# Gate rows summed by TensorE inside the norm transitions, and twelve modulation units of four rows of 512 in feed-forward blocks zero and one

## The reference, cut to what matters

```python
sh1, sc1, gt1, sh2, sc2, gt2 = split(silu(c) @ w_ada + b_ada, 6)
x = x + gt1 * mixer(rmsnorm(x, g_mix) * (1 + sc1) + sh1)
x = x + gt2 * swiglu(rmsnorm(x, g_ffn) * (1 + sc2) + sh2)     # feed-forward block zero
x = rmsnorm(x, g_final)
(sh1, sc1, g1, sh2, sc2, g2, sh3, sc3, g3) = split(silu(c_2) @ w_ada_2 + b_ada_2, 9)
x = x + 0.5 * g1 * swiglu(mod(x, sh1, sc1))                   # feed-forward block one
x = x + g2 * (attention_mixer(mod(x, sh2, sc2)) @ w_out_2)
x = x + 0.5 * g3 * swiglu(mod(x, sh3, sc3))                   # feed-forward block two
out = rmsnorm(x, final_norm_2)
```

## Time and profile before

| | us |
|---|---|
| median of 3 runs (1157.52 to 1158.29) | 1157.75 |
| profiled execution, its own time from first to last instruction (the span) | 1156.4 |
| TensorE busy with matmuls / weight loads | 1118.4 / 1008.5 |
| VectorE, ScalarE, POOL busy | 853.4, 571.7, 74.7 |
| HBM traffic | 250.29 MB, mean 216 GB/s |

### The profile page before, as it was taken

How to read it: one execution, slowest core, us unless ns; L and a number is a source line. 1 busy time by engine, 2 the same in 40 slices (tenths; PEclk the granted TensorE clock), 3 DMA queues, 4 the chain that set the end, 5 groups by cost and what they waited for, 6 DMA issues and landing times.

```text
span 1156.4 us, 19131 instructions
## 1 busy us (share of the span) xinstructions
PE 1118.4 (97%) x7744; PEld 1008.5 (87%) x7744; DVE 853.4 (74%) x1082; ACT 571.7 (49%) x733; POOL 74.7 (6%) x143
## 2 busy tenths in 40 slices
PE   2999999999999999999999999999999999999997
PEld 2899988999999888888788888889999998888885
DVE  1578766897777688877888778878777776755676
ACT  3495434544434644445454454446655546444442
POOL 4000000100000100000200000011000001000001
PEclk8899999999999999999999999999999999999999
DMA  9934554688875488778468777747965654655771
GB/s 287 291 114 140 188 175 154 183 273 263 296 233 187 154 282 272 238 247 293 154 226 271 252 258 263 239 152 240 292 183 182 222 178 165 218 182 191 234 247 37
DMA packets 192548, 250.29 MB, mean 216 GB/s; under 512 B 4859, under 2 KB 171966, under 8 KB 192350
## 3 DMA queue, kind: packets, MB, share of 16 engines
q1 hardware_dynamic: 183838, 216.92, 57.8%
q0 software_dynamic: 8640, 32.38, 8.4%
HBM read 248.23 MB, written 1.05 MB: 216 GB/s over the span
## 4 chain that ended last, share of the span: by engine, by line
PE 87%; DVE 7%; ACT 2%; SPq 2%; DMA 1%; issue 1%; POOL 0%; POOLq 0%; DVEq 0%; ACTq 0%
PE twin L1291 85%; DVE wlo L1912 2%; DVE arena L1920 2%; DMA arena<-in_w_ada 1%; DVE arena L1912 1%; ACT arena L862 1%; DVE X L1912 1%; ACT whi L862 1%; PE twin L1628 1%; SPq L520 1%; SPq L570 0%; DVE arena L1916 0%; PE twin L1749 0%; PE twin L1416 0%; DVE B_lo L1912 0%
## 5 line engine op out<-in xcount | busy, mean ns | idle before, releaser
L1291 PE MATMUL twin<-A_both,whi 128*128 128x256 f32 (+1 forms) x2208 | 578.7, 339 | 3.1 <-DVE A_both L1912 1.6
L1912 DVE TENSOR_TENSOR wlo<-raw,whi 128x2048 fp32r<-128x2048 f32 (+1 forms) x171 | 386.9, 2263 | 117.1 <-ACT whi L862 117.0
L1291 PE MATMUL twin<-A_both,wlo 128*128 128x256 f32 x1632 | 436.5, 280 | 0.0
L862 ACT ACTIVATE whi<-raw 128x2048 fp32r<-128x2048 f32 x169 | 323.2, 1913 | 206.8 <-PE twin L1291 205.7
L1291 PEld LDWEIGHTS twin<-A_both,whi 128*128 128x128 f32 x2208 | 370.1, 190 | 46.1 <-issue 7.9
L1291 PEld LDWEIGHTS twin<-A_both,wlo 128*128 128x128 f32 x1632 | 309.2, 189 | 11.4 <-DVE A_both L1912 0.6
L1920 DVE SCALAR_TENSOR_TENSOR arena<-ada_raw,arena 128x256 f32<-128x256 f32 (+2 forms) x322 | 167.3, 520 | 15.9 <-issue 1.7
L862 ACT ACTIVATE arena<-twin 128x512 f32<-128x512 f32 (+5 forms) x171 | 90.8, 556 | 111.5 <-PE twin L1291 81.9
L862 ACT ACTIVATE arena<-arena 128x512 f32<-128x512 f32 (+7 forms) x132 | 69.9, 559 | 149.1 <-DVE arena L1912 116.0
L1291 PE MATMUL twin<-whi,B_hi 128*128 128x512 f32 (+2 forms) x340 | 126.6, 372 | 0.2 <-DVE B_lo L1912 0.2
L1291 PE MATMUL twin<-wlo,B_hi 128*128 128x512 f32 (+2 forms) x340 | 125.1, 368 | 0.0
(11 more groups left out here) (137 smaller groups left out, 900.6 us busy)
## 6 DMA issues: line engine op xcount, KB each, us to landing
raw<-in_w_in SPq DMA_DIRECT2D x48, 1024.0 KB, 5.7
raw<-in_ffn_w_in SPq DMA_DIRECT2D x44, 1024.0 KB, 5.1
ada_raw<-in_w_ada POOLq DMA_DIRECT2D x28, 1024.0 KB, 6.0
ada_raw<-in_w_ada SPq DMA_DIRECT2D x24, 1024.0 KB, 5.4
raw<-in_w_ffn_in SPq DMA_DIRECT2D x22, 1024.0 KB, 5.1
raw<-in_ffn_w_out SPq DMA_DIRECT2D x22, 1024.0 KB, 5.0
raw<-in_w_ffn_out SPq DMA_DIRECT2D x11, 1024.0 KB, 5.0
arena<-in_w_ada SPq DMA_DIRECT2D x8, 1024.0 KB, 11.8
```

What stands on the lines that cost most here:

```text
L862: return nc.scalar.activation(o, i, f, **kw)
L1291: return nc.tensor.matmul(o, l, r, start=start, stop=stop, **kw)
L1912: return nc.vector.tensor_tensor(o, x, y, op)
```

## The change

The gate sums leave their five places. `gate_half(r, 0)` runs in the norm transition behind `shift_and_scale`, `gate_half(r, 1)` behind the transposes, each in a bank that stays untouched until `gate_row(r)` has read it; r = 1, 2, 3, 4 go to norm 2, 3, 4, 5, and r = 0 behind the transposes of the last ga unit. `gate_row` of r = 1, 2, 4 moves on DVE from the end of the block to its beginning, that of r = 3 to the third unit of the second mixer; it now waits for `gr_in` itself. TensorE waits for `gr_done` in the middle of the second up unit of each block and before uq. The `keep_warm` products go, but for eight in norm 3. The column sums move to bank 0 (bank 7 for norm 4). All modulation units become half pairs of four rows of 512; blocks zero and one take twelve each, at the slots `ADA_STEP` (1, 3, 6, 8, 11, 13, 16, 18, 21, 23, 26, 28, counted three to a step), block two none. SP and DVE write all steps out; ACT and PE keep the loops, now also for all of block two.

```diff
@@ -113,22 +113,19 @@
     ADA += [(_blk, _col * D + 256 * n) for n in range(4)]
-NADA1, NADAF, NADA2 = 16, 10, 12
+NADA1, NADAF, NADA2 = 16, 12, 12
 ADA_P2 = NADA1 + 2 * NADAF
-ADA_LAST = ADA_P2 + NADA2
+ADA_STEP = [1 + 5 * j // 2 for j in range(NADAF)]
 MOD_STEP = {4: 0, 5: 1, 7: 2, 9: 3, 11: 4, 13: 5, 16: 6, 18: 7, 21: 8, 24: 9, 26: 10, 28: 11, 30: 12, 32: 13, 34: 14, 36: 15}
-ADA_FFN = [n for n in range(len(ADA)) if NADA1 <= n < ADA_P2 or n >= ADA_LAST]
+ADA_FFN = [n for n in range(len(ADA)) if NADA1 <= n < ADA_P2]
 ADA_MIX = [n for n in range(len(ADA)) if n not in ADA_FFN]
-LAST_STEPS = (0, NF - 4, NF - 3, NF - 2)
-
-
 def ada_pos(n):
-    return n if n < NADA1 else n - NADA1 if n < ADA_P2 else n - ADA_P2
+    return n if n < NADA1 else (n - NADA1) % 20
@@ -462,14 +459,11 @@
-        def feed_forward_steps(eng, f, step):
-
-            end = NF - 1 if f < 2 else NF - 4
-            with eng.Fori(0, (end - 1) // 3) as j:
+        def feed_forward_steps(eng, step):
+
+            with eng.Fori(0, (NF - 2) // 3) as j:
                 for m in range(1, 4):
                     step((j, m), m)
-            for i in range(end, NF - 1):
-                step(i, i)
@@ -498,13 +492,10 @@
         def ada_source(n):
-            if ADA_P2 <= n < ADA_LAST:
-                blk, c0 = ADA[n - n % 2]
-                k = 4 * (n % 2)
-                return a["w_ada_2"][0].rearrange("(p k) n -> p k n", k=KD)[:, k:k + 4, c0:c0 + 2 * UC]
-            blk, c0 = ADA[n]
-            w = a["w_ada"][0] if blk == 0 else a["w_ada_2"][0]
-            return w.rearrange("(p k) n -> p k n", k=KD)[:, :, c0:c0 + UC]
+            blk, c0 = ADA[n - n % 2]
+            k = 4 * (n % 2)
+            w = a["w_ada"] if blk == 0 else a["w_ada_2"]
+            return w[0].rearrange("(p k) n -> p k n", k=KD)[:, k:k + 4, c0:c0 + 2 * UC]
@@ -534,32 +525,28 @@
-                def piece(a, i, b, n):
-
-                    if isinstance(i, tuple):
-                        return bass.ds(lin(a, i, b), n)
-                    return slice(a * i + b, a * i + b + n)
-
-                def step(i, m):
-                    load(u0 + 2, i, w_in[:, :, piece(UC, i, UC, UC)], KD)
-                    load(u0 + 3, i, w_in[:, :, piece(UC, i, DFF + UC, UC)], KD)
-                    load(u0 + 4, i, w_out[:, piece(2, i, 0, 2), :], 2)
-                    if f < 2:
-                        n0 = NADA1 + NADAF * f
-                        blk, c0 = ADA[n0 + m]
-                        w = (a["w_ada"] if blk == 0 else a["w_ada_2"])[0].rearrange("(p k) n -> p k n", k=KD)
-                        if n0 == NADA1 and m == 0:
-                            sp.wait_ge(*ada_done(n0 - 1))
-                        else:
-                            sp.wait_ge(ada_mac, lin(KD, i, KD * ada_order(n0)))
-                        sp.dma_start(ada_raw[:], w[:, :, piece(UC, i, c0 - UC * m, UC)]).then_inc(ada_landed, 16)
-                    elif m in LAST_STEPS and i == m:
-                        load_ada(ADA_LAST + LAST_STEPS.index(m))
+                def next_ada(q):
+
+                    if f < 2 and q in ADA_STEP[:-1]:
+                        load_ada(NADA1 + NADAF * f + ADA_STEP.index(q) + 1)
+
+                def step(i):
+                    cs = slice(UC * i + UC, UC * i + 2 * UC)
+                    load(u0 + 2, i, w_in[:, :, cs], KD)
+                    next_ada(3 * i - 4)
+                    load(u0 + 3, i, w_in[:, :, DFF + UC * i + UC:DFF + UC * i + 2 * UC], KD)
+                    next_ada(3 * i - 3)
+                    load(u0 + 4, i, w_out[:, 2 * i:2 * i + 2, :], 2)
+                    if f < 2 and i == 0:
+                        load_ada(NADA1 + NADAF * f)
+                    next_ada(3 * i - 2)
                 load(u0, 0, w_in[:, :, 0:UC], KD)
                 load(u0 + 1, 0, w_in[:, :, DFF:DFF + UC], KD)
-                step(0, 0)
-                feed_forward_steps(sp, f, step)
+                step(0)
+                for i in range(1, NF - 1):
+                    step(i)
+                next_ada(3 * (NF - 1) - 4)
                 load(u0 + 3 * NF - 1, 0, w_out[:, 2 * (NF - 1):2 * NF, :], 2)
@@ -638,11 +625,11 @@
-            return 7 if n in (3, 4) else 3
-
-        def gate_bank(r):
-
-            return {0: 6, 3: 2}.get(r, 4)
+            return 7 if n == 4 else 0
+
+        def gate_bank(r, x):
+
+            return ((2, 3), (3, 4), (7, 3), (1, 3), (3, 5))[r][x]
@@ -780,7 +767,7 @@
                     pool.wait_ge(unit_used, 1)
-                pool.dma_start(ada_half if n >= ADA_P2 else ada_raw[:], ada_source(n)).then_inc(ada_landed_p, 16)
+                pool.dma_start(ada_half, ada_source(n)).then_inc(ada_landed_p, 16)
@@ -1341,12 +1328,17 @@
                 src = norm_source(n)
+                r = n - 1
+                if n == 3:
+                    pe.wait_ge(x_piece, 1)
                 shift_and_scale(n, column_bank(n))
-                warm = {2: 4, 5: 5}.get(n, 3)
+                if n == 4:
+                    pe.wait_ge(x_piece, 6)
+                gate_half(r, 0)
+                if n == 3:
+                    keep_warm(6, 8)
                 for t in range(TT):
-                    if t == 0:
-                        keep_warm(7 if n in (2, 5) else 6, {2: 4, 3: 16}.get(n, 5))
-                    else:
+                    if t:
                         turn_sums(n, column_bank(n))
@@ -1358,17 +1350,21 @@
                             ins.then_inc(tr_done, 1)
-                keep_warm(warm, 3)
-
-            def gate(r):
+                if n in (3, 4):
+                    pe.wait_ge(x_piece, 4 * (n - 2))
+                else:
+                    pe.wait_ge(x_ready, 1 if n == 2 else 5)
+                gate_half(r, 1)
+
+            def gate_half(r, x):
                 g0 = GATE_UNITS[r]
-                pe.wait_ge(*ada_done(g0 + 3))
-                pe.wait_ge(gr_in, 16 * (r + 1))
-                for x in range(2):
-                    c = UC * ada_pos(g0) + 512 * x
-                    ins = mm(bank[gate_bank(r) + x][:], ones[:], acc[:, c:c + 512], True, True)
-                ins.then_inc(gr_mm, 1)
+                if x == 0:
+                    pe.wait_ge(*ada_done(g0 + 3))
+                c = UC * ada_pos(g0) + 512 * x
+                ins = mm(bank[gate_bank(r, x)][:], ones[:], acc[:, c:c + 512], True, True)
+                if x:
+                    ins.then_inc(gr_mm, 1)
@@ -1548,10 +1544,12 @@
-                def up(u, i, b):
+                def up(u, i, b, gates=0):
                     pe.wait_ge(lo_ready, lin(3, i, u + 1))
                     for half in range(2):
+                        if half and gates:
+                            pe.wait_ge(gr_done, gates)
                         for k in range(KD):
@@ -1592,14 +1590,13 @@
                 first_up(u0, 0, low_count(2 + f + (f == 2)))
-                up(u0 + 1, 0, 2)
+                up(u0 + 1, 0, 2, (2, 3, 5)[f])
                 up(u0 + 2, 0, 4)
                 up(u0 + 3, 0, 6)
                 pe.wait_ge(prod_done, n0 + 1)
                 down(u0 + 4, 0, 0, True, False)
-                feed_forward_steps(pe, f, step)
+                feed_forward_steps(pe, step)
                 pe.wait_ge(prod_done, n0 + NF)
-                gate((1, 2, 4)[f])
                 down(u0 + 2, NF - 1, NF - 1, False, True)
@@ -1659,13 +1656,12 @@
                     s = ring(u)
-                    if (kind, n) == ("out2", 0):
-                        gate(3)
                     pe.wait_ge(lo_ready, u + 1)
                     wait_banks(n2, BEFORE2[n2][:1] if (kind, n) == ("bra", 0) else BEFORE2[n2], EV2)
                     if kind in ("uq", "ukv"):
                         k0, nk, w = (0, 2, 768) if kind == "uq" else (2, 1, 1024)
                         pe.wait_ge(lat_lo, 1)
+                        pe.wait_ge(gr_done, 4)
                         wh = whi[s][:, 0:nk * w].rearrange("p (k w) -> p k w", k=nk)
@@ -1858,8 +1854,6 @@
                 b = BANKS1[u]
-                if kind == "mix_out" and n == 0:
-                    gate(0)
                 pe.wait_ge(lo_ready, u + 1)
@@ -1889,6 +1883,9 @@
                     ins.then_inc(ont_tr, 1)
+                    if n == 3:
+                        gate_half(0, 0)
+                        gate_half(0, 1)
             norm(2)
@@ -1938,26 +1935,13 @@
-            def adapt(n, i, dst, blk):
-
-                s = 0 if blk == 0 else 2
-                arrived, count = ada_landing(n)
-                dve.wait_ge(arrived, lin(16, i, count))
-                for k in range(KD):
-                    if k:
-                        dve.wait_ge(ada_mac, lin(KD, i, KD * ada_order(n) + k))
-                        ins = stt(dst, ada_raw[:, k, :], c3[:, k, s:s + 1], dst, ALU.mult, ALU.add)
-                    else:
-                        ins = ts(dst, ada_raw[:, k, :], c3[:, k, s:s + 1], None, ALU.mult)
-                    ins.then_inc(ada_mac, 1)
-
-            def adapt_half(n):
-
-                m, h = n - n % 2, n % 2
```

(44 more changed lines are left out.)

4 lines of the change are left out of this document (2 added, 2 removed).

## The result

The changed kernel takes 1151.71 us in the median of four runs (1151.33 to 1152.92), against 1157.86 of the kernel before beside it (1157.52 to 1158.29): a ratio of 0.9949, 95% interval 0.9937 to 0.9961. It is faster by about 6 us. The forecast was 1152.9, range 1151.0 to 1157.5.

The account below looks back on a forecast made before the run. TensorE's matmuls, 97% of the span, were taken as the bound. Gains of 4.1, 1.1 and 0.3 less losses of 0.2 and 0.4 gave 4.9 us off 1157.75: 1152.9 us, range 1151.0 to 1157.5.

Parts of the forecast that it names:

- gate pairs, three blocks: Ends of the feed-forward blocks: removing the ones matmuls saves 1.2 us each in blocks zero and one, 1.72 in two.
- second mixer, out2 and uq: Second mixer: the moved row operation delays uq by 0.93 us, out2 gains 0.47; a loss of 0.4 to 0.5.
- gate pair at mix_out: First mixer, row zero: the pair only moves, mix_out may wait for a low part; loss 0 to 0.42, taken 0.2.
- first steps: First step of each feed-forward block: shorter or no adapt removes TensorE's 0.36 us wait, 1.1 us in all.
- tight slots: Eight places right before product in blocks zero and one: modulation unit fits by 0.05 to 0.3 us, costing nothing.
- mask, and 249 us: First mixer, before inside_chunks: the shorter adapt gains at most the 0.27 us wait for the mask, summed as 0.3.
- norm transitions: Gate matmuls replace keep-warm products where TensorE idles: cost nothing; if late by 0.2 us in each of four, 0.8.
- gate rows at the head of a block: gate_row adds 1.2 us to VectorE at each block's start, covered by waits or margin; at most 3.6 if uncovered.
- rival (a): The slots just before product fail eight times; at 0.9 us each 1160.1 us, slower; chance in full 0.09.
- Rival (b): Gate pairs were hidden, the down product starts late for another reason: about 1157.0 us; chance 0.2, shared with partial rival (a).
- rival (d): Transition to block one: fewer warming products let the clock fall, 8.4 us lost, time 1161.4 us; chance 0.03.
- rival (c): Everything hides: no mixer losses, slots before product fine, full 1.72 us in all three blocks: 1151.0 us; chance 0.08.

Follow-up runs that it names:

- gates back: The changed kernel with gate pairs, their row operations and the keep-warm products back at their former places: 1155.28 us, ratio to the kernel before 0.998.
- The run with one operation more: The changed kernel with one more 128x512 VectorE operation behind the modulation operation at each of eight slots in blocks zero and one: 1157.21 us.

## Why the prediction was right, step by step

| step | forecast | measured | from |
|---|---|---|---|
| gate pairs, three blocks | -4.1 | -4.1 | changed against gates back |
| second mixer, out2 and uq | +0.46 | +0.55 | the same |
| gate pair at mix_out | +0.2 | +0.17 | from 37 us to block zero, changed against gates back |
| first steps | -1.1 | -0.60, -0.64, -0.68 | gates back against before, less its tight slots |
| tight slots | 0 | +0.15 and +0.65 | steps over 16.63 us, blocks zero and one |
| mask, and 249 us | -0.3 | -0.46 | start distances, 37 to 250 us |
| norm transitions | 0 | 0 | last product before to first behind: 6.52, 9.66, 6.58, 6.52 before; 6.53, 9.67, 6.59, 6.53 changed |
| gate rows at the head of a block | 0 | 0 | first step 28.03 in blocks zero and two, changed and gates back |

From 37 us to the last store issue the forecast was 4.9, and the two traces of the changed kernel give 4.93 and 5.05. Two errors of 0.8 us and opposite sign cancelled in it: that the sum came out so well is luck.

*First steps*, the term that was mis-sized: "3 x 0.36 = 1.1 us" took the idle time from the wait as it is listed. It was 1.9. The text ahead of the prediction says that a matmul costs the distance of starts; I used that for the gate pairs, which came out to 0.1 us, and not for the waits.

*Tight slots*, the step that failed: "It fits by 0.05 to 0.3 us, and costs nothing as long as nothing slips." In block zero the chain of sums was right to 0.1 us, and the margin was nothing: steps of 16.69 where 16.62 is free. In block one it slipped, by something that I had not looked for: GpSimd's copies, which the order of the code puts beside three of the four tight operations. The run with one operation more confirms the mechanism of rival (a), where each further 0.7 us costs 0.70. It would have decided the sign from 0.6 us each, as priced; the changed kernel stood at 0.1 each.

*Gate pairs.* Rival (b) is refuted: the pair was on the path, 1.18 where a low part ends the wait and 1.75 where nothing does. TensorE starts 0.15 behind the low part, as read from the uq unit. *Row three* behaved as priced: uq waits 1.11 instead of 0.17. At mix_out the low part comes at 359.38 instead of 358.06, ends at 360.07, and TensorE starts at 360.12, where its rhythm of 0.12 would give 360.05: a wait too short to be listed. That 0.07 and 0.10 for the restart are the 0.17. A wait of this kind also stood in the kernel before at 248.69 us, behind a modulation operation; it cost 0.14 and the change removed it, which the prediction didn't price: so the stretch ahead of mix_out gained 0.46 and not 0.3.

*The clock*, rival (d): TensorE idles 1.23 us before the transposes and the granted clock stays at the upper level (2.4 GHz); at 3.01 us it falls. The Trainium skill (TensorE: Matmul & The Clock Gate, HAM oscillation) warns that idle times between bursts bring the lower clock back; the trace agrees for the idle time of 3.01 us and not for the shorter ones. So the eight products that the change kept are worth their place. The fall cost about 0.35 us in the trace, far from the 8.4 that I took from the start of the kernel, because only 3.4 us ran at the lower level, beside waits. The 8.4 was no price in the first place: it is clock that was not granted, counted over 60 us in which TensorE had matmuls for 37.12.

*VectorE without loops* cost nothing that can be seen: its only idle time put down to issue is 1.54 us at 907.44, the one of 1.68 in the earlier trace rows. *Outside the steps* I priced nothing. About 1.1 of the 6.1 us lie there, 0.6 at the very end (in every trace with the new units) and 0.5 ahead of 37 us, which is within the scatter of that start. Neither was taken apart.

*Small slips.* 580.09 plus two units of 5.7 is 591.5 and not 591.7, 554.53 + 2.20 is 556.73 and not 556.77, the terms of rival (c) give 1151.2 and not 1151.0, and those of (d) 1161.3 and not 1161.4. Among TensorE's waits one of 0.4 us for `wlo` in the second mixer was left out. None of this changes a conclusion; that wait is as long in both kernels.

## What to carry to other kernels

Price a wait by the distance of starts around it, plus the slower restart; on a pipelined engine the idle time shown leaves out the overlap (0.36 shown, 0.6 to 0.7 lost), and a loss of 0.3 can show none. When work is moved into a slot whose margin is a few tenths, look at every engine that works in that slot and not only at the chain you sum, and prefer a place ahead of an operation that waits for someone else: the same 0.7 us cost 0.70 behind the last split and 0.07 ahead of it. Cut traces at fixed starts: most stages repeated to 0.1 us where medians moved by 0.5.

## What the runs showed of the hardware

- A GpSimd copy (128x256) beside VectorE's modulation operations of 128x512 takes 1.06 us (0.79 beside the shorter first one of a sum) instead of 0.66 to 0.68, and four of VectorE's take 3.54 instead of 3.31. Beside the additions of 128x512 that read one input from a bank of PSUM the copy takes 0.66 to 0.68 as well (603.02 and 617.12). Beside a split, which reads two tiles of SBUF, it takes 2.59 us. The Trainium skill (SBUF — State Buffer, Who interferes with whom) says that the two share one port pair, which one of them holds alone. The trace agrees: the split lost nothing, and the copy ended 0.53 us behind it; where both were delayed, the delays add up to 0.6 us, nearly one copy.
- TensorE's first matmul of 512 columns after a wait takes 0.30 to 0.33 to the next start instead of 0.23, even after a gap as short as 0.24 us.
- An idle time of 1.23 us left the granted clock at 2.4 GHz, one of 3.01 us was followed by 1.2 GHz for some 3.4 us.
